# The split weights of every product block placed on a multiple of 128 bytes in SBUF

## What is computed

```python
# first block
h = rms_norm(x, norm1);  proj = h @ w_in                  # 1024 x 5128
o_a = forgetting_attention(...);  o_b = chunk_band_attention(...)
merged = g_a * (o_a @ w_branch_a) + g_b * (o_b @ w_branch_b)
x = x + merged @ w_out
x = rms_norm(x + square(relu(rms_norm(x, norm2) @ w_up)) @ w_down, final_norm)   # hidden 4096
# second block, layer 0: gated linear attention and RWKV-7 recurrence; layer 1: MLA attention
for i in range(2):
    h = even_mixer(x, ...) if i == 0 else odd_mixer(x, ...)
    x = layer_norm(DN_ALPHA * x + h, ...)
    x = layer_norm(DN_ALPHA * x + swiglu_ffn(x, ...), ...)                        # hidden 2816
```

## The kernel before

| block | built in | time in the trace, us | PSUM banks of a plain tile | first slot, bytes | beyond a multiple of 128 |
|---|---|---|---|---|---|
| 1 | `first_attentions` | 17 to 335 | 0 to 5, later 0 and 1 | 161344 | 64 |
| 2 | `mix_and_ffn` | 335 to 1011 | 0 to 5, later 0 and 1 | 154976 | 96 |
| 3 | `even_out_to_mla` | 1170 to 1880 | 0 to 5, later 0 and 1 | 150944 | 32 |
| 4 | `odd_out` | 1882 to 2305 | 2 to 7 | 160000 | 0 |

## Time and profile before

### The profile page before, as it was taken

One profiled execution on the slowest core, in us unless ns is written; L12 is line 12 of the kernel. 1 busy time (PEld: TensorE's weight loads), 2 busy tenths in 40 slices (PEclk: granted clock), 3 DMA queues, 4 the chain that ended last, 5 costly groups with the idle time before them and its releaser, 6 DMA issues. The chain is left out here.

```text
span 2331.5 us, 35424 instructions
## 1 busy us (share of the span) xinstructions
PE 2238.7 (96%) x14855; PEld 1828.7 (78%) x14855; DVE 1009.1 (43%) x1598; ACT 855.8 (37%) x1510; POOL 246.8 (11%) x307
## 2 busy tenths in 40 slices
PE   8999999999999999979999999999999989999997
PEld 7777667888888887757768888888777778888886
DVE  5343336354343345556466433334443345333333
ACT  5443443342232244244334222222465534222223
POOL 4000000000000011013325000001321114000001
PEclk9999999999999999999999999999999999999998
DMA  5312123233333223200013333333242022333320
GB/s 165 91 52 58 46 64 99 73 100 91 100 91 91 80 75 100 64 11 3 3 50 91 92 108 91 99 91 88 62 90 56 10 82 87 100 95 100 100 82 37
DMA packets 346617, 178.64 MB, mean 77 GB/s; under 512 B 44054, under 2 KB 340164, under 8 KB 346460
## 3 DMA queue, kind: packets, MB, share of 16 engines
q1 hardware_dynamic: 344428, 171.54, 26.1%
q0 software_dynamic: 2032, 4.85, 0.7%
HBM read 171.35 MB, written 2.11 MB: 74 GB/s over the span
## 5 line engine op out<-in xcount | busy, mean ns | idle before, releaser
L428 DVE TENSOR_TENSOR w_lo<-w,w_hi 128x1024 fp32r<-128x1024 f32 (+2 forms) x327 | 400.7, 1228 | 429.7 <-ACT w_hi L421 429.4
L445 PE MATMUL bank<-act_hi,w_hi 128*128 128x512 f32 (+1 forms) x1480 | 565.1, 382 | 12.0 <-DVE act_lo L1050 5.2
L447 PE MATMUL bank<-act_hi,w_lo 128*128 128x512 f32 (+1 forms) x1480 | 549.0, 371 | 0.0
L446 PE MATMUL bank<-act_lo,w_hi 128*128 128x512 f32 (+1 forms) x1480 | 547.0, 370 | 0.0
L421 ACT ACTIVATE w_hi<-w 128x1024 fp32r<-128x1024 f32 (+2 forms) x328 | 337.0, 1030 | 361.0 <-PE bank L447 249.9
L445 PEld LDWEIGHTS bank<-act_hi,w_hi 128*128 128x128 f32 x1480 | 280.8, 190 | 71.1 <-issue 17.4
L447 PEld LDWEIGHTS bank<-act_hi,w_lo 128*128 128x128 f32 x1480 | 280.6, 190 | 50.7
L446 PEld LDWEIGHTS bank<-act_lo,w_hi 128*128 128x128 f32 x1480 | 281.4, 190 | 47.0 <-issue 1.0
L445 PE MATMUL bank<-hid_hi,w_hi 128*128 128x512 f32 (+1 forms) x560 | 208.3, 372 | 0.0
L447 PE MATMUL bank<-hid_hi,w_lo 128*128 128x512 f32 (+1 forms) x560 | 207.5, 371 | 0.0
L446 PE MATMUL bank<-hid_lo,w_hi 128*128 128x512 f32 (+1 forms) x560 | 206.9, 370 | 0.0
(11 more groups left out here) (460 smaller groups left out, 2913.0 us busy)
## 6 DMA issues: line engine op xcount, KB each, us to landing
w<-in_ffn_w_gate_up SPq DMA_DIRECT2D x88, 512.0 KB, 3.8
w<-in_w_in SPq DMA_DIRECT2D x41, 512.0 KB, 3.9
w<-in_w_up SPq DMA_DIRECT2D x32, 512.0 KB, 4.0
w<-in_w_down SPq DMA_DIRECT2D x32, 512.0 KB, 4.0
w<-in_ffn_w_down SPq DMA_DIRECT2D x32, 512.0 KB, 3.9
w<-in_even_w_in SPq DMA_DIRECT2D x28, 512.0 KB, 3.8
w<-in_ffn_w_down SPq DMA_DIRECT2D x16, 384.0 KB, 3.4
w<-in_w_out SPq DMA_DIRECT2D x8, 512.0 KB, 4.0
```

The lines of the kernel that those rows point to most:

```text
L428: e.tensor_tensor(w_lo[:, 0:part.n], w.raw[part.g % w.LOADS][:, 0:part.n], w_hi[:, 0:part.n].bitcast(F32), ALU.subtract).then_inc(w.lo.sem, 1)
L445: e.matmul(s.acc, *first, start=(k == 0), stop=False)
L446: e.matmul(s.acc, *second, start=False, stop=False)
L447: last = e.matmul(s.acc, *third, start=False, stop=(k == kt - 1))
```

## The change

A function `on_boundary` looks at the place that the SBUF stack has reached and allocates an unused tile up to the next multiple of `size` bytes. `Gemm.__init__` calls it with 128 ahead of the ten (or eight) slots. The gap is 64 bytes in block 1, 32 in block 2, 96 in block 3; in block 4 there is none, since the stack stands on a multiple of 128 already. What is allocated after the slots in the same scope moves by the same bytes: `gla_last` and `gla_stat` in block 2, and `rope_cos`, `rope_sin`, `rope_rate` and `rope_sign` in block 3. All other tiles keep their places. The instructions of every engine, their order, their shapes and their waits are the same as before.

| block | first slot before | first slot after | after, beyond a multiple of 256 | after, beyond a multiple of 512 |
|---|---|---|---|---|
| 1 | 161344 | 161408 | 128 | 128 |
| 2 | 154976 | 155008 | 128 | 384 |
| 3 | 150944 | 151040 | 0 | 0 |
| 4 | 160000 | 160000 | 0 | 256 |

```diff
+def on_boundary(core, ctx, name, size):
+
+    gap = -(-(-core.nc.sbuf_base // 32) * 32) % size
+    if gap:
+        core.sb(ctx, name, [P, gap // 4])
 
 
 def constants(core, A):
...
         self.core, self.ctx, self.weights, self.jobs, self.early = core, ctx, core.weights, jobs, first_parts
         self.given = given
         self.SLOTS = slots
+        on_boundary(core, ctx, "w_gap", 128)
         self.w_hi = [core.sb(ctx, f"w_hi{r}", [P, KD * P], F32R) for r in range(self.SLOTS)]
         self.w_lo = [core.sb(ctx, f"w_lo{r}", [P, KD * P], F32R) for r in range(self.SLOTS)]
```

## The result

The changed kernel takes 2326.09 us (median of 4 runs, 2323.35 to 2328.3) against 2337.37 us before in the same runs: a ratio of 0.9949, interval 0.9935 to 0.9963. Timed again in a later set of runs it is 0.9943 (0.9926 to 0.9961). It is faster, but by 11.3 us, and lies just above the range of the forecast. The profiled execution took 2324.24 us, its span is 2322.2 us.

A forecast was written before the change was run, and what follows sets the result against it. TensorE was taken to bound the kernel through distances between matmul starts. Gains of 33.1 (stationary weights) and 1.2 (moving), less 0.4 (256 columns) and 1.4 (mixed work), took 32.5 us off 2336.8: 2304.3, rounded to 2304.5, range 2299 to 2326.

The forecast's parts named there:

- What bounds the kernel: Whole span: TensorE, busy 96%, alone sets the end, so the time is a sum of distances between matmul starts.
- The failing step: Stationary weights, blocks 1 and 2: matmul distances fall to block 4's 226.6 ns, gaining 4.9 and 15.7 us.
- Block 3's term: Stationary weights in block 3: 1920 matmuls gain 6.5 ns each by the matched pair with block 4, 12.5 us.
- The sum: Whole kernel: 33.1 + 1.2 - 0.4 - 1.4 = 32.5 us faster.
- Block 2's term: Stationary weights in block 2: 2094 matmuls go from 234.1 to 226.6 ns, 7.5 ns each, 15.7 us.
- block 1's: Stationary weights in block 1: 711 matmuls go from 233.5 to 226.6 ns, 6.9 ns each, 4.9 us.
- A fifth off for mixed work: Products alternating with attention, blocks 1 to 3: of 7.1 us at risk to longer waits, 1.4 us is lost.
- Weights moving: `TokenJob` products in blocks 1 to 3: gain between nothing and 2.4 us, half taken, 1.2 us.
- The other period: Weights' addresses: if only multiples of 256 bytes count, block 3 alone gains 12.5 us, giving 2324; chance 0.09.
- The slower rival: Weights' place relative to the moving tile, modulo 512, counts: three blocks out of phase, 14.1 us more, 2351; chance 0.05.
- Nothing changes: Block 4 is faster for another reason than its weights' place, so the time stays 2336.8; chance 0.10.
- The distance to the median: Profiled span against timed runs: the median stands 5.3 us above the span, and this distance is kept.

The follow-up runs named there:

- e5: The kernel before, unchanged, profiled a second time as the control for the clock; 2335.28 us.
- e2: The changed kernel with the split weights of all four blocks 128 bytes beyond a multiple of 256; 2339.73 us in one run.
- e4: The changed kernel with block 4's moving tiles alone 128 bytes off, weights of blocks 1 to 4 at 0, 64, 192, 0 beyond 256; 2331.02 us.
- e8: The changed kernel with weights 32, 160, 32, 192 bytes beyond a multiple of 256 in blocks 1 to 4; block 4's 1392 matmuls took 318.3 us.
- e3: The changed kernel with block 4's activations, hidden tiles and weights all 128 bytes off, weights of blocks 1 to 3 at 64, 32, 64; 2333.74 us.
- e6: The changed kernel with block 4's activations, hidden tiles and weights 32 bytes off, weights of blocks 1 to 3 at 224, 192, 224; block 4's run 315.3 us.
- e9: The changed kernel with weights starting inside one tile per block, at distances 4, 8, 240 and 16 bytes in blocks 1 to 4; 2330.56 us.

## Why the forecast was wrong

**What bounds the kernel**: right. The whole difference lies in distances between matmul starts; no new wait on weights came up in the pure stretches, and the splits kept their price.

**The failing step** is "The distance goes from 232.6 to 234.4 (I take 233.5) down to 226.6", and likewise "from 234.1 to 226.6" for block 2. It took for granted that a multiple of 128 is what block 4 has. Block 4 has a distance of zero modulo 256 from its moving tiles, and the change gave that to block 3 alone. Before, the distances were 64, 96, 160 and 0 in blocks 1 to 4; after, 128, 128, 0 and 0. In its place the runs show 232.4 ns in one execution and 233.4 in another for block 1, which had 233.3 (nothing to 0.9 ns gained, instead of 6.9), and 1.1 us on block 2's 1284 matmuls (300.5 to 299.4), 0.9 ns each, or 1.8 us for the 2094 instead of 15.7. The forecast saw that no row had weights 128 bytes beyond a multiple of 256 and gave this case 0.09. With one fast block at an address that was a multiple of 128 and of 256 alike, the trace had no grounds for preferring 128.

**Block 3's term** held in the long run: 324.5 to 315.3 us is 6.6 ns a matmul, 12.7 us if all 1920 gained it, against 12.5. What the 528 others gained was not measured by itself. By the starts in the traces, the matmuls from 1605.9 to 1882.0 us of the kernel before took 276.6 and 276.3 us in its two profiles and 275.0 in the changed kernel's first, with 12 to 13 us of the lower clock in each.

**The sum.** 12.7 + 1.8 is 14.5 us, if every product gained as in the long runs, of which 11.3 are in the medians and 13.4 in the second timing (2337.18 less 2323.74). The products with moving weights gave some back (0.3 us in 96 of them, below), those in mixed work gained less, and the times vary by several us from one execution to another.

**What the mechanism would have given**: with all blocks in place the gain is 27.1 and 27.3 us, where 32.5 were forecast for that state. Block 2's term is then right in kind (9.6 us on 1284 matmuls is 7.5 ns each, as forecast), and so is block 1's in its pure run (233.3 to 226.8 ns, 6.5 each, for 6.9 forecast). Part of what fell short is block 1's mixed work. Between 80 and 320 us, where products alternate with attention, the same window holds 1308 and 1310 matmuls in the two profiles of the kernel before, 1311 after and 1314 with all on 256; the last two rows:

```profile
80.00:320.00 240.00, 234.40 (x1311) 172.59 (x1309) 90.91 (x222) 100.91 (x242) 0.00 (x0) 1.00 0.20 53
```

```profile
80.00:320.00 240.00, 234.31 (x1314) 173.06 (x1313) 91.53 (x223) 101.62 (x243) 0.00 (x0) 1.00 0.20 53
```

Four to six matmuls more in 1308 are 0.7 to 1.1 us, where 470 products by 6.9 ns would be 3.2. A fifth off for mixed work was too little there; whether waits for softmax took the rest, or neighbours that are no such pair, was not tested.

**Weights moving**: the rows of the 96 matmuls in block 1, for the kernel before (second profile), the changed one and all on 256:

```profile
71.20:93.00 21.80, 21.80 (x97) 17.89 (x96) 4.90 (x4) 6.84 (x9) 0.00 (x0) 1.00 0.41 107
```

```profile
70.60:92.70 22.10, 22.10 (x97) 17.90 (x96) 4.90 (x4) 6.78 (x9) 0.00 (x0) 1.00 0.40 108
```

```profile
70.00:91.50 21.50, 21.50 (x96) 17.83 (x95) 4.90 (x4) 6.74 (x9) 0.00 (x0) 1.00 0.42 110
```

The change made them 3 ns slower, a loss that the forecast's lower end of zero had left out; in place they gain over 2 ns. The starts in the traces give the distances: 229.1, 232.3 and 226.7 ns. The kept traces also show why. In these products the weights are the moving operand, so stationary minus moving is the other way round: block 1's weights at 64 give 192, and 192 cost 228.9 ns with the weights stationary. The last section has all such pairs.

**The rivals.** The other period was right in size (12.5 us) and in the block it named, and wrong in its cause: it spoke of the weights' own address. The slower rival named the true quantity, the place relative to the moving tile, with the wrong modulus (512) and so the wrong sign. "Nothing changes" fell. The Trainium skill (page "SBUF — State Buffer", section "Specifications (TRN2)") gives SBUF lines of 16 bytes and a penalty for each access that crosses to a new one. The traces do not agree with it as the whole rule: bases that are all multiples of 16 bytes differ by up to 7.5 ns a matmul (226.7 to 234.2).

**The distance to the median.** The forecast kept 5.3 us between span and median; the changed kernel's own profile shows 2.0 us between its span and its time, and so does e5 with 1.7. The first profile of the kernel before was therefore one of its quick executions, by the same 2 us at about 2333.5. The gain that was forecast does not hang on it.

## What to carry to other kernels

For float32r products with 512 moving columns, place the stationary and the moving tile at the same offset modulo 256 bytes in a partition, high and low parts alike; it is the difference that counts, with its sign, so moving either will do. When a natural experiment has a single good case, list every modulus and every difference that the good case satisfies before choosing one, and check which of them the change gives to the others. Long runs of products at full clock repeated within 0.2 us between executions of one kernel where times varied by several: compare those, and for a short run read the starts.

## What the runs showed of the hardware

The distance between starts of 512-column matmuls by (stationary minus moving) modulo 256 bytes, from the long runs. A dash is a distance that no run had there. Four bytes, tried in block 1 alone, gave 232.4 ns where the same block has 233.3 at 64 bytes and 226.8 at zero, by 142 distances each.

| distance, bytes | block 2, ns | blocks 3 and 4, ns |
|---|---|---|
| 0 | 226.7 | 226.7 |
| 8 | 230.6 | - |
| 16 | - | 233.3 |
| 32 | 233.4 | 233.4 |
| 64 | 233.3 | 233.4 |
| 96 | 234.2 | - |
| 128 | 233.4 | 232.4 (e2 block 3, e4 block 4), 233.3 (e2 block 4) |
| 160 | 233.4 | 233.4 |
| 192 | 228.9 | 228.9, 228.8 |
| 224 | - | 233.4 |
| 240 | - | 228.3 |

The cost is no smooth function: 192 and 240 are cheap, 224 is not. At 128 bytes the same block 4 gave 233.3 ns with the weights moved and 232.4 with the activations moved. That need not be the placement: block 1 of the changed kernel gave 232.4 in one execution and 233.4 in another. What picks between the two values at 128 is not known.

Products with moving weights (`TokenJob`) fit the same table when the sign is kept. The kept traces have 96 of them in a row in block 1 and 174 in block 2; the distances are worked out from the starts in the traces, those of block 2 without the few outside 200 to 260 ns.

| weights beyond a multiple of 256, bytes | stationary minus moving | weights moving, ns | the same distance in the table above, ns |
|---|---|---|---|
| 0 | 0 | 226.7 (block 1), 227.6 (block 2) | 226.7 |
| 32 | 224 | 233.3 (e8 block 1), 233.3 (e3 block 2) | 233.4 |
| 64 | 192 | 229.1 (before, block 1), 229.2 (e4 block 2) | 228.9 |
| 96 | 160 | 233.4 (before, block 2) | 233.4 |
| 128 | 128 | 232.3 (after, block 1), 232.9 (after, block 2) | 232.4 to 233.4 |
| 160 | 96 | 234.2 (e8 block 2) | 234.2 |
| 192 | 64 | 233.2 (e6 block 2) | 233.3 |
| 224 | 32 | 233.3 (e6 block 1) | 233.4 |
| 4 | 252 | 236.5 (e9 block 1) | - |
| 8 | 248 | 233.4 (e9 block 2) | - |

The sign matters: 64 bytes cost 233.3 ns one way and 229 the other, in both kinds of product.

Products with 256 moving columns showed no such cost: 108 of them took 12.80 us at a distance of 160 as at zero.
